# First shift and scale by TensorE in halves of 512 features, and q, k, v in halves of the contraction, in a two-layer fp32 transformer kernel

## The chip, the cores and the metric

The kernel runs on one core of a Trainium2 chip, as one launch. The metric is device time in microseconds (us). A core has TensorE (PE in the profile, with PEld for its weight loads), VectorE (DVE), ScalarE (ACT), GpSimd (POOL) and SyncE (SP), which here only issues DMAs. Each runs its own program in order, and semaphores tie them together.

## The reference

Two layers over 256 tokens of 1024 features, in float32. What matters here is the start of the first layer:

```python
mod = c @ w_ada[l] + b_ada[l]                        # c: 1 x 1024, w_ada: 1024 x 6144
sh1, sc1, gt1, sh2, sc2, gt2 = jnp.split(mod, 6, axis=-1)
h = modulate(rms_norm(x, g_pre_mix[l]), sh1, sc1)    # h * (1 + sc1) + sh1
proj = h @ w_in[l]
bg, cg, u, q, k, v, ga, gb = jnp.split(proj, ...)    # 512 columns each, ga and gb 1024
```

q, k and v feed a stick-breaking attention of 8 heads, bg, cg and u a short convolution, ga and gb gate the two. An output projection, an MLP, and then a second layer with sparse attention and a gated MLP follow. `sh1` and `sc1` are needed before the first product, `gt1` only after the first layer's `w_out`.

## The kernel before, in words

**Products.** Each large product is done in chunks of 1 MB of weights, numbered p = 0, 1, 2 and so on. SP brings chunk i of a list named `plan` into one of four `raw` buffers (L555); a buffer is used again when its last reader has let go. ACT writes `w_hi`, the chunk rounded to fp32r (`high`, L1126), DVE writes the rest, `w_lo = raw - w_hi` (`low`, L1517), and TensorE adds up three passes: w_hi by act_hi, w_hi by act_lo, w_lo by act_hi (`passes`, L596). `w_hi` and `w_lo` have three slots each, so `high(p)` waits until product p - 3 is done. After each product p, ACT and DVE take up chunk p + 3 (`high_after`, `low_after`). A product with 256 columns of weights is 8 tiles of contraction x 2 blocks x 3 passes = 48 matmuls with 256 moving columns into one bank of PSUM.

**The first products.** `in1_order` runs q, k, v (two chunks of 256 columns each, p = 0 to 5), then c, u, b, ga and gb (p = 6 to 19). Every product needs all 1024 features of h. The heads' work stands between products from p = 6 on: scores at L711, transposes at L721, outputs at L735.

**Shift and scale.** All six vectors of `mod` are made alike. DVE multiplies each row tile of `w_ada` by its element of c and adds it to `mod_acc` (L1506, L1509), two instructions of 1024 columns for each 1 MB chunk. Four chunks make one vector; TensorE then adds over the partitions with `ones` (`modulation_sum`, L633) and DVE adds the bias (`modulation`, L1545). The eight chunks of SCALE1 and SHIFT1 stand first in the plan, ahead of product 0; the other sixteen stand behind products (`n % 2`, that is after 1, 3, 5, ... 23, and four in the MLP).

**The start.** TensorE turns x, adds its squares (L642), and fills in with matmuls of the identity (`keep_busy`, L665). ACT takes the root (L1138), scales x by the scale (L1162), splits products 0 and 1, and then adds the shift and rounds to `act_hi` (L1168). POOL multiplies by the reciprocal root (L2154). DVE makes `act_lo` (L1576).

The order on ACT there, in code:

```python
high(0)
high(1)
act.wait_ge(mod_set, 2)
for k in range(DT):
    act.wait_ge(y_normed, k + 1)
    e.activation(act_hi[:, k, :], wide[1][:, k, :], ACT.Identity,
                 bias=mod[:, SHIFT1 * DT + k:SHIFT1 * DT + k + 1]).then_inc(tiles_hi, 1)
preload(ACT.Sigmoid)
```

Of the kernel before, what the change touches and what calls it, by code (L numbers as in the profile page):

```python
# [15 lines left out]
P = 128  # L16
# [54 lines left out]
def build(nc, a, out):  # L71
# [30 lines left out]
    with fixed:  # L102
# [14 lines left out]
        eps, scratch1, mean_of, rstd_out = (singles[:, 0:1], singles[:, 1:2], singles[:, 2:3], singles[:, 4:4 + TT])  # L117
# [145 lines left out]
        for name, width in (("b", CONV), ("c", CONV), ("u", CONV), ("q", ATTN), ("k", ATTN), ("v", ATTN),  # L263
# [3 lines left out]
        in1_order = [(name, i) for name in ("q", "k", "v", "c", "u", "b", "ga", "gb")  # L267
                     for i in range(in1[name].shape[1] // CHUNK_COLS)]
# [12 lines left out]
        ada_order = [(v, r) for v in (SCALE1, SHIFT1, GATE1, SHIFT2, SCALE2, GATE2) for r in range(ADA_CHUNKS)]  # L281
# [10 lines left out]

        GATE2_WITH = tuple(MLP1 + 7 + i * 10 // (ADA_CHUNKS - 1) for i in range(ADA_CHUNKS))
# [10 lines left out]
        def plan_product(source):  # L304
            n = len(product_at)
            product_at.append(len(plan))
            plan.append(("w", n, source))
            if n % 2 and n < 6 * ADA_CHUNKS or n in GATE2_WITH:
                plan_ada()

        for _ in range(2 * ADA_CHUNKS):
            plan_ada()
        for name, i in in1_order:
            plan_product(in1[name][:, i * CHUNK_COLS:(i + 1) * CHUNK_COLS])
# [32 lines left out]
        steps = [i for i, item in enumerate(plan) if item[0] != "ada"]  # L347
# [6 lines left out]
        def raw_view(i):  # L354
# [16 lines left out]
        gains_set, y_scaled, y_normed = sem("gains_set"), sem("y_scaled"), sem("y_normed")  # L371
# [40 lines left out]
        down_half, down_added, gain_applied, close_squared, bias_set = (  # L412
            sem(n) for n in ("down_half", "down_added", "gain_applied", "close_squared", "bias_set"))
# [15 lines left out]
        squared_by = (5, 9, 13)  # L429

# [26 lines left out]
        for i in range(DT // 2):  # L457
            banks.use(("x", i), squared, i + 1)
        banks.use(("mod", SCALE1), mod_set, 1)
        banks.use("rows1", cols_set, 2)  # L460
        banks.use("rows2", cols_set, 3)
        banks.use(("mod", SHIFT1), mod_set, 2)
        evacuated = {"q": qk_copied, "k": qk_copied, "v": v_copied, "c": c_copied, "u": u_gated, "b": b_copied,
                     "ga": gated, "gb": gated}
        counted = {}
        for p, (name, i) in enumerate(in1_order):
            s = evacuated[name]
            counted[id(s)] = counted.get(id(s), 0) + 1
            banks.use(p, s, counted[id(s)])
            if p == 2 * ADA_CHUNKS - 1:  # L470
                banks.use(("mod", GATE1), mod_set, 3)
# [8 lines left out]
        banks.use(("mod", SHIFT2), mod_set, 4)  # L480
        banks.use(("mod", SCALE2), mod_set, 5)
# [3 lines left out]
        for i in range(DT // 2):  # L485
            banks.use(("mlp_out", i), branch2_set, 2 * i + 2)
            if i == 0:
                banks.use(("mod", GATE2), mod_set, 6)
# [48 lines left out]
        mod_no = {v: n for n, v in enumerate((SCALE1, SHIFT1, GATE1, SHIFT2, SCALE2, GATE2))}  # L537
# [4 lines left out]
        def sync_program(e):  # L542
# [20 lines left out]
        def tensor_program(e):  # L563
# [42 lines left out]

            def product_low_last(p, o, hi, lo, ready):

                for parts in ((0, 1), (2,)):
                    for k in range(DT):  # L610
                        passes(p, o, hi, lo, ready, k, 0, True, True, parts=parts)
# [79 lines left out]
            for i in range(DT // 2):  # L691
                sum_tiles((2 * i, 2 * i + 1), i == 0, i == DT // 2 - 1, (squared, i + 1))
            keep_busy(8, bank[O_BANK])
# [45 lines left out]

            for p, (name, i) in enumerate(in1_order):  # L740
                step = p - 6
# [10 lines left out]
                if p in (1, 2):  # L752
# [1524 lines left out]
```

## Time and profile before

| | |
|---|---|
| time, median of 3 runs | 771.2 us (770.83 to 771.45) |
| span of the profiled execution | 769.0 us |
| time less span, taken for the profiled execution too | 2.2 us |
| PE busy | 737.8 us (96%) |
| DVE, ACT, POOL busy | 508.3 us (66%), 369.1 us (48%), 80.3 us (10%) |
| mean granted TensorE clock | 0.981 |
| read from HBM | 144.57 MB |

The span runs from the first to the last instruction; the profile gives no other time for its execution, so its own time is taken as the span plus the 2.2 us. Busy time is the sum over the span. A matmul on plain float32 operands is run as two instructions, so eight such matmuls stand as x16. The end of a matmul is modelled and overlaps the start of the next, so the price of one in a row is the distance between starts.

### The profile page before, as it was taken

Reading aid. Unit: us, or ns where it says so; the run is one execution under the profiler, and the core shown is the slowest. Engines: PE = TensorE matmul, PEld = TensorE weight load, DVE = VectorE, ACT = ScalarE, POOL = GpSimd, SP = SyncE. Lnnn points to the kernel's source line nnn. Section 1 sums busy time; section 2 is a strip of 40 time slices with the busy share of each in tenths; the row PEclk is TensorE's granted clock in tenths of the full one; section 3 lists DMA queues with packets and bytes.
Section 4 is the critical chain, followed back from the end, with each engine's and each line's share of the span. In section 5 each row is a group of like instructions: output and inputs, shape, how many; then the busy total and the mean of one; then the engine's idle time right before and its main releaser. Section 6 shows DMA issues by size and latency. Waiting matters only on the chain.

```text
span 769.0 us, 13566 instructions
## 1 busy us (share of the span) xinstructions
PE 737.8 (96%) x5881; PEld 703.9 (92%) x5881; DVE 508.3 (66%) x609; ACT 369.1 (48%) x508; POOL 80.3 (10%) x76
## 2 busy tenths in 40 slices
PE   4899999999999999999999999998899999999996
PEld 4899999999999999999999999786699999999884
DVE  4998689687575777754446989865655665556361
ACT  3453444444545455534336365676654544444341
POOL 1500111003000000000014000013000322221001
PEclk9799999999999999999999989999899999999998
DMA  9989866877605777766551551605334665664511
GB/s 341 375 284 326 273 203 209 284 279 226 222 5 190 246 225 250 239 223 214 173 169 55 181 170 35 196 24 177 97 107 141 214 217 176 216 187 170 190 57 55
DMA packets 118335, 146.49 MB, mean 191 GB/s; under 512 B 4004, under 2 KB 103556, under 8 KB 118276
## 3 DMA queue, kind: packets, MB, share of 16 engines
q1 hardware_dynamic: 116912, 143.58, 56.7%
q10 hardware_dynamic: 1364, 2.05, 0.8%
q8 instruction: 46, 0.75, 0.4%
q14 instruction: 13, 0.11, 0.0%
HBM read 144.57 MB, written 1.05 MB: 189 GB/s over the span
## 4 chain that ended last, share of the span: by engine, by line
PE 77%; DVE 15%; ACT 4%; DMA 2%; issue 2%; POOLq 0%; SPq 0%; DVEq 0%; ACTq 0%
PE bank L596 56%; PE bank L1087 8%; DVE w_lo L1517 6%; ACT w_hi L1126 3%; DVE mod_acc L1509 3%; PE bank L778 3%; DMA raw<-in_w_ada 2%; DVE wide L1786 1%; PE bank L878 1%; PE bank L880 1%; PE bank L656 1%; PE bank L633 1%; PE bank L858 1%; PE bank L897 1%; PE bank L642 1%
## 5 line engine op out<-in xcount | busy, mean ns | idle before, releaser
L1517 DVE TENSOR_TENSOR w_lo<-raw,w_hi 128x2048 fp32r<-128x2048 f32 x108 | 243.3, 2258 | 119.3 <-ACT w_hi L1126 119.2
L1126 ACT ACTIVATE w_hi<-raw 128x2048 fp32r<-128x2048 f32 x110 | 206.9, 1885 | 222.2 <-PE bank L596 175.8
L596 PE MATMUL bank<-act_hi,w_hi 128*128 128x256 f32 x816 | 228.1, 281 | 0.4 <-ACT act_hi L1283 0.3
L596 PE MATMUL bank<-act_lo,w_hi 128*128 128x256 f32 x816 | 225.9, 279 | 1.4 <-DVE act_lo L1808 0.7
L596 PE MATMUL bank<-act_hi,w_lo 128*128 128x256 f32 x816 | 222.0, 278 | 0.0
L596 PEld LDWEIGHTS bank<-act_hi,w_hi 128*128 128x128 f32 x816 | 154.2, 189 | 3.4 <-issue 2.8
L596 PEld LDWEIGHTS bank<-act_lo,w_hi 128*128 128x128 f32 x816 | 153.3, 188 | 2.3 <-DVE act_lo L1808 0.9
L596 PEld LDWEIGHTS bank<-act_hi,w_lo 128*128 128x128 f32 x816 | 151.2, 188 | 0.0
L596 PE MATMUL bank<-ffn_hi,w_hi 128*128 128x256 f32 x352 | 98.1, 279 | 0.0
L596 PE MATMUL bank<-ffn_hi,w_lo 128*128 128x256 f32 x352 | 97.4, 277 | 0.6 <-DVE w_lo L1517 0.6
L596 PE MATMUL bank<-ffn_lo,w_hi 128*128 128x256 f32 x352 | 97.3, 277 | 0.0
L596 PE MATMUL bank<-hidden_hi,w_lo 128*128 128x256 f32 x256 | 70.8, 277 | 0.9 <-DVE w_lo L1517 0.9
L596 PE MATMUL bank<-hidden_hi,w_hi 128*128 128x256 f32 x256 | 71.0, 277 | 0.0
L596 PE MATMUL bank<-hidden_lo,w_hi 128*128 128x256 f32 x256 | 70.7, 276 | 0.0
L596 PEld LDWEIGHTS bank<-ffn_hi,w_lo 128*128 128x128 f32 x352 | 66.2, 188 | 0.8 <-DVE w_lo L1517 0.8
L596 PEld LDWEIGHTS bank<-ffn_lo,w_hi 128*128 128x128 f32 x352 | 66.1, 188 | 0.1
L596 PEld LDWEIGHTS bank<-ffn_hi,w_hi 128*128 128x128 f32 x352 | 66.1, 188 | 0.1
L1509 DVE SCALAR_TENSOR_TENSOR mod_acc<-raw,col_tile,mod_acc 128x1024 f32<-128x1024 f32 x42 | 55.3, 1318 | 2.4 <-DMA raw<-in_w_ada 1.2
L596 PEld LDWEIGHTS bank<-hidden_hi,w_lo 128*128 128x128 f32 x256 | 48.1, 188 | 1.1 <-DVE w_lo L1517 1.1
L596 PEld LDWEIGHTS bank<-hidden_lo,w_hi 128*128 128x128 f32 x256 | 48.1, 188 | 0.0
L596 PEld LDWEIGHTS bank<-hidden_hi,w_hi 128*128 128x128 f32 x256 | 48.1, 188 | 0.0
L2226 POOL TENSOR_TENSOR wide<-wide,rstd 128x512 f32<-128x512 f32 x11 | 28.9, 2625 | 143.8 <-ACT wide L1466 143.8
(277 smaller groups left out, 1101.7 us busy)
## 6 DMA issues: line engine op xcount, KB each, us to landing
raw<-in_w_in SPq DMA_DIRECT2D x31, 1024.0 KB, 6.1
raw<-in_w_ada SPq DMA_DIRECT2D x24, 1024.0 KB, 6.3
raw<-in_w_gate_up SPq DMA_DIRECT2D x22, 1024.0 KB, 5.1
raw<-in_w_mlp_in SPq DMA_DIRECT2D x16, 1024.0 KB, 5.4
raw<-in_w_mlp_out SPq DMA_DIRECT2D x16, 1024.0 KB, 5.2
raw<-in_w_down SPq DMA_DIRECT2D x10, 1024.0 KB, 5.1
raw<-in_w_out SPq DMA_DIRECT2D x8, 1024.0 KB, 7.0
raw<-in_w_proj_conv SPq DMA_DIRECT2D x2, 1024.0 KB, 6.0
```

What stands on the lines that cost most here:

```text
L596: i = e.matmul(dst, lhs, rhs, start=start and k == 0 and (m == 0 or second is not None) and n == 0, stop=stop and k == kt - 1 and n == 2, ...
L633: i = e.matmul(o[:, k * HD:(k + 1) * HD], acc[:, k * P:(k + 1) * P], ones[:, 0:HD], start=True, stop=True, skip_group_check=True)
L642: i = e.matmul(bank[SUMS][:, 0:T], ones[:], squares[:, k, :], start=first and n == 0, stop=last and n == len(tiles) - 1, skip_group_check= ...
L656: t = e.matmul(bank[SUMS][:, tt * HD:(tt + 1) * HD], squares[:, k, tt * P:(tt + 1) * P], mean_of.to_broadcast([P, HD]), start=k == 0 and t ...
L778: t = e.matmul(o[:, m * T:(m + 1) * T], wp[:, k, cut], ap[:, k, :], start=k == 0 and m == 0 and n == 0, stop=k == kt - 1 and n == 2, skip_ ...
L858: t = e.transpose(b[:, i * P:(i + 1) * P], score[h % IN_FLIGHT][:, at * P:(at + 1) * P], ident[:])
L878: e.matmul(b[:, 0:keys], q2[:, h, tt * P:(tt + 1) * P], ks_T[:, g, 0:keys], start=False, stop=False, skip_group_check=True)
L1087: i = e.matmul(outs[tt][:, 0:n_cols], ap[:, k0 + k, own_], wp[:, k, :], start=first and k == 0 and n == 0, stop=last and k == kt - 1 and n ...
L1126: e.activation(w_hi[slot][:, 0:kt * n_cols], raw[i % N_RAW][:, 0:kt * n_cols], ACT.Copy).then_inc(hi_split, 1)
L1509: t = e.scalar_tensor_tensor(out=acc[:], in0=src[:, k, :], scalar=cols("c", r * ADA_TILES + k, 1), in1=acc[:], op0=ALU.mult, op1=ALU.add)
L1517: e.tensor_tensor(w_lo[slot][:, 0:kt * n_cols], raw[i % N_RAW][:, 0:kt * n_cols], w_hi[slot][:, 0:kt * n_cols].bitcast(F32), ALU.subtract) ...
L2226: e.tensor_tensor(s_, s_, rstd_2, ALU.mult).then_inc(gate_pool, 1)
```

## The change

The eight chunks of SCALE1 and SHIFT1 no longer go through DVE. Each is now 512 rows x 512 columns of `w_ada` (1 MB), in the order scale, shift for features 0 to 511, then the same for 512 to 1023. For each, `feed_mod1` runs four matmuls of 512 moving float32 columns straight from `raw`, whose weights are an element column of c spread over 32 columns, each into its own 32 partitions of one bank. DVE copies the bank (`copy_mod1`), and `pick_mod1` turns it to a column and adds the four groups by four matmuls with 8 moving columns. The bias and the `1 +` are added by DVE from there. The first four chunks stand ahead of product 0, the other four ahead of product 3.

Products 0 to 5 become q, k, v over the first 512 rows of the contraction and then q, k, v over the last 512, each 512 columns wide, in six banks. q and k use 256 moving columns as before; v has 512 moving columns. Product 0 runs its three passes one after the other over all its tiles. On ACT, `high(2)` stands ahead of the second half of scale and shift, and `high(3)` behind it; on DVE `low(3)` stands behind it. The multiplication by the reciprocal root moves from POOL (8 instructions of 256 columns) to DVE (4 of 512), ahead of the first copy. The other sixteen `w_ada` chunks stay on DVE; twelve of them move from behind products 1, 3, ... 23 to behind 6, 8, 10, 12, 14, 16, 17, 18, 19, 20, 21, 22, and the sum for GATE1 from after product 7 to after product 12.

```diff
-        in1_order = [(name, i) for name in ("q", "k", "v", "c", "u", "b", "ga", "gb")
-                     for i in range(in1[name].shape[1] // CHUNK_COLS)]
+        in1_order = [(name, i) for i in range(2) for name in ("q", "k", "v")]
+        in1_order += [(name, i) for name in ("c", "u", "b", "ga", "gb")
+                      for i in range(in1[name].shape[1] // CHUNK_COLS)]
...
+        first_mod = [(half, v, r) for half in range(2) for v in (SCALE1, SHIFT1) for r in range(2)]
+        ADA_WITH = (6, 8, 10, 12, 14, 16, 17, 18, 19, 20, 21, 22)
...
+                    elif before == "mod":
+                        sp.wait_ge(mod1_fed, m + 1)
...
+            def feed_mod1(n):
+                half, v, r = first_mod[n]
+                o, i = bank[MOD1_BANKS[half][n // 2 % 2]], mod_at[n]
...
+                for j in range(HALF_ROWS):
+                    t = e.matmul(o[32 * j:32 * (j + 1), :], cols("c", r * HALF_ROWS + j, 1).to_broadcast([P, 32]),
+                                 raw_view(i)[:, j, :], start=r == 0, stop=r == 1, skip_group_check=True)
+                t.then_inc(mod1_fed, 1)
+            def pick_mod1(m):
+                o = bank[MOD1_BANKS[m // 2][m % 2]]
+                pe.wait_ge(*mod1(f"copied{m}"))
+                for k in range(HALF_ROWS):
+                    t = e.matmul(o[:, k * 8:(k + 1) * 8], mod1_rows[m][:, k * P:(k + 1) * P], pick.to_broadcast([P, 8]),
+                                 start=True, stop=True, skip_group_check=True)
+                t.then_inc(mod1_picked, 1)
+            keep_busy(4, bank[O_BANK])
+            feed_mod1(0)
             keep_busy(8, bank[O_BANK])
-            modulation_sum(SCALE1)
+            feed_mod1(1)
             transpose_rows(1)
             transpose_rows(2)
-            keep_busy(30, bank[O_BANK])
-            modulation_sum(SHIFT1)
-            keep_busy(5, bank[O_BANK])
+            pick_mod1(0)
+            feed_mod1(2)
+            keep_busy(8, bank[O_BANK])
+            feed_mod1(3)
+            keep_busy(4, bank[O_BANK])
+            pick_mod1(1)
+            keep_busy(6, bank[O_BANK])
...
+            for part in range(3):
+                half_product(0, Q_BANKS, 0, (part,), by_row)
+            half_product(1, K_BANKS, 0, (0, 1, 2), by_row)
+            feed_mod1(4)
+            feed_mod1(5)
+            half_values(2, 0, between={(0, 2): partial(pick_mod1, 2), (1, 0): feed_shift, (1, 3): partial(pick_mod1, 3)})
+            half_product(3, Q_BANKS, 1, (0, 1, 2), by_row)
+            half_product(4, K_BANKS, 1, (0, 1, 2), by_bank)
+            half_values(5, 1)
...
# ACT
+            scale_half(0)
             high(0)
+            shift_half(0)
+            preload(ACT.Sigmoid)
             high(1)
+            high(2)
+            scale_half(1)
+            shift_half(1)
...
# DVE
             reciprocal(0)
+            for i in range(DT // 2):
+                e.tensor_tensor(wide[1][:, s2, :], x_T[:, s2, :], rstd_2, ALU.mult).then_inc(y_normed, 1)
+            copy_mod1(0)
             transpose_rows(1)
             transpose_rows(2)
+            scale_half(0)
+            copy_mod1(1)
+            shift_half(0)
+            first_low(0)
+            stream_to(product_at[2])
+            copy_mod1(2)
+            scale_half(1)
+            copy_mod1(3)
+            shift_half(1)
+            first_low(1)
...
             for p, (name, i) in enumerate(in1_order):
+                if p < 6:
+                    low_after(product_at[p])
+                    if p >= 3:
+                        first_copies(p)
+                    continue
```

## Rows read from the trace of the kernel before

**Rows 1.** The page: busy time, and the granted TensorE clock in 40 slices.
```profile
PE 737.8 (96%) x5881; PEld 703.9 (92%) x5881; DVE 508.3 (66%) x609; ACT 369.1 (48%) x508; POOL 80.3 (10%) x76
...
PEclk9799999999999999999999989999899999999998
```

**Rows 2.** The chain that ended last in time: start, length, what.
```profile
2.94 12.58 DMA raw<-in_w_ada
...
38.16 34.41 PE bank L596 x287
72.57 0.86 PE bank L711 x8
...
701.14 60.44 PE bank L1087 x264
```

**Rows 3.** Timeline of the start: start, length, engine, line, instruction.
```profile
13.64 1.95 PE L665 MATMUL bank<-ident 128*128 128x128 f32 x16
...
15.19 0.47 ACT L1138 ACTIVATE rms<-bank,singles 128x256 f32<-128x256 f32 x1
...
20.78 1.75 DVE L1550 RECIPROCAL rstd<-rms 128x256 f32<-128x256 f32 x1
...
20.92 3.67 PE L633 MATMUL bank<-ones,mod_acc 128*128 128x64 f32 x16 [5.33 <-DVE mod_acc L1509]
...
27.64 3.30 ACT L1162 ACTIVATE wide<-x_T,scale 128x256 f32<-128x256 f32 x8 [11.98 <-DVE scale L1567]
...
34.26 1.90 PE L633 MATMUL bank<-ones,mod_acc 128*128 128x64 f32 x16
...
36.66 3.46 ACT L1168 ACTIVATE act_hi<-wide,mod 128x256 fp32r<-128x256 f32 x8 [0.55 <-DVE mod L1545]
```

**Rows 4.** Stretches: length, busy time and instructions of each engine, granted clock, DMA share, GB/s.
```profile
18.00:20.00 2.00, 0.00 (x0) 0.00 (x0) 1.86 (x3) 0.00 (x0) 0.00 (x0) 1.00 1.03 410
20.00:22.00 2.00, 1.08 (x5) 1.08 (x6) 2.00 (x2) 0.00 (x0) 0.00 (x0) 0.51 1.03 410
```

**Rows 5.** One stretch, instructions of L596 alone: PE, PEld, clock, DMA.
```profile
44.14:72.34 28.20, 28.20 (x242) 28.20 (x240) 1.00 0.99 334
```

**Rows 6.** Groups by form: busy us, mean ns | idle before, releaser.
```profile
L1517 DVE TENSOR_TENSOR w_lo<-raw,w_hi 128x2048 fp32r<-128x2048 f32 x105 | 240.4, 2295 | 114.6 <-ACT w_hi L1126 114.5
...
L1742 DVE TENSOR_TENSOR x_T<-x_T,wide 128x512 f32<-128x512 f32 x8 | 5.5, 702 | 0.0
...
L1769 DVE SCALAR_TENSOR_TENSOR act_lo<-wide,mod,act_hi 128x256 fp32r<-128x256 f32 x8 | 3.6, 476 | 0.0
...
L1126 ACT ACTIVATE w_hi<-raw 128x2048 fp32r<-128x2048 f32 x107 | 204.4, 1914 | 215.1 <-PE bank L596 175.8 <-PE bank L1087 16.9 <-DMA raw<-in_w_in 13.6
L1116 ACT ACT_TABLE_LOAD x11 | 14.1, 1283 | 0.2
```

**Rows 7.** Timeline of PE around one L735 at 95 us; the second answer ends at 95.40.
```profile
94.92 0.49 PE L721 MATMUL bank<-ident,weight 128*128 128x128 f32 x3
95.34 0.87 PE L735 MATMUL bank<-weight_T,v_nat 128*64 128x256 f32 x8
96.14 0.39 PE L596 MATMUL bank<-act_hi,w_hi 128*128 128x256 f32 x1
...
95.34 0.44 PE L735 MATMUL bank<-weight_T,v_nat 128*64 128x256 f32 x2
```

**Rows 8.** Timeline of PE, plain float32 weights chunk as moving operand.
```profile
480.85 1.95 PE L914 MATMUL bank<-raw,cmp_in 128*79 128x256 f32 x8
```

**Rows 9.** DMA issues: KB each, median us from issue to landing.
```profile
raw<-in_w_ada SPq DMA_DIRECT2D x24, 1024.0 KB, 6.3
```

**Rows 10.** Timeline of DVE where the moved chunks will stand, and that stretch.
```profile
154.54 0.69 DVE L1610 TENSOR_TENSOR mixed_lo<-conv_y,mixed_hi 128x512 fp32r<-128x512 f32 x1 [4.03 <-ACT mixed_hi L1206]
155.15 2.60 DVE L1509 SCALAR_TENSOR_TENSOR mod_acc<-raw,col_tile,mod_acc 128x1024 f32<-128x1024 f32 x2
...
160.00:170.00 10.00, 10.00 (x87) 10.00 (x87) 8.22 (x6) 5.33 (x5) 0.00 (x0) 1.00 1.03 379
```

More of the change, by code:

```diff
@@ L280, in build @@
         ADA_CHUNKS = DT // ADA_TILES
[L281 removed]
+        ada_order = [(v, r) for v in (GATE1, SHIFT2, SCALE2, GATE2) for r in range(ADA_CHUNKS)]
+        first_mod = [(half, v, r) for half in range(2) for v in (SCALE1, SHIFT1) for r in range(2)]
         IN1, PC = 0, 20
@@ L536, in build @@
         S_BANKS, T_BANK, O_BANK = (4, 5), 6, 7
-        mod_no = {v: n for n, v in enumerate((SCALE1, SHIFT1, GATE1, SHIFT2, SCALE2, GATE2))}
+        mod_no = {v: n for n, v in enumerate((GATE1, SHIFT2, SCALE2, GATE2))}
+        mod1_rows = [mod_acc[n // 2][:, n % 2 * HALF_COLS:(n % 2 + 1) * HALF_COLS] for n in range(4)]
         EXT_I, ROWS_SET, TABLES, K_ROWS, Q_BASE = 2, 10, 18, 22, 23
@@ L738, in stick_output, with half_product @@
                             t.then_inc(stick_out, 1)
+            def half_product(p, outs, half, parts, order, between={}):
+                for n_at, (j, k) in enumerate(order):
+                    if n_at in between:
+                        between[n_at]()
+                    kt, n_cols = tiles_of(p)
+                    wh = w_hi[p % N_SPLIT][:].rearrange("p (k c) -> p k c", k=kt)
+                    wl = w_lo[p % N_SPLIT][:].rearrange("p (k c) -> p k c", k=kt)
+                    row = half * HALF_ROWS + k
+                    for m in range(CHUNK_COLS // P):
+                        cut = slice(j * CHUNK_COLS + m * P, j * CHUNK_COLS + (m + 1) * P)
+                        for n, (wp, ap) in enumerate(((wh, act_hi), (wh, act_lo), (wl, act_hi))):
+                            if n not in parts:
+                                continue
+                            if n == 0:
+                                pe.wait_ge(hi_split, p + 1)
+                                pe.wait_ge(*ready_h1[row][0])
+                            elif n == 1:
+                                pe.wait_ge(*ready_h1[row][1])
+                            else:
+                                pe.wait_ge(*low_ready(p))
+                            t = e.matmul(bank[outs[j]][:, m * T:(m + 1) * T], wp[:, k, cut], ap[:, row, :],
+                                         start=row == 0 and m == 0 and n == 0, stop=row == DT - 1 and n == 2,
+                                         skip_group_check=True)
+                if 2 in parts:
+                    t.then_inc(product_done, 1)
@@ new lines, in half_values @@
+            def half_values(p, half, between={}):
+                outs = [start_bank(("v", tt)) for tt in range(TT)]
+                kt, n_cols = tiles_of(p)
+                wh = w_hi[p % N_SPLIT][:].rearrange("p (k c) -> p k c", k=kt)
+                wl = w_lo[p % N_SPLIT][:].rearrange("p (k c) -> p k c", k=kt)
+                for tt in range(TT):
+                    for k in range(kt):
+                        if (tt, k) in between:
+                            between[tt, k]()
+                        row = half * HALF_ROWS + k
+                        for n, (ap, wp) in enumerate(((act_hi, wh), (act_lo, wh), (act_hi, wl))):
+                            if n == 0:
+                                pe.wait_ge(hi_split, p + 1)
+                                pe.wait_ge(*ready_h1[row][0])
+                            elif n == 1:
+                                pe.wait_ge(*ready_h1[row][1])
+                            else:
+                                pe.wait_ge(*low_ready(p))
+                            t = e.matmul(outs[tt][:, 0:n_cols], ap[:, row, tt * P:(tt + 1) * P], wp[:, k, :],
+                                         start=row == 0 and n == 0, stop=row == DT - 1 and n == 2, skip_group_check=True)
+                    if row == DT - 1 and tt == 0:
+                        t.then_inc(token_half, 1)
+                t.then_inc(product_done, 1)
```

211 lines of the change are left out of this document (130 added, 81 removed).

## The prediction, made before the changed kernel was seen

> **What bounds the kernel now.** The page comes first: TensorE is busy 96% of the span [rows 1], so only two things can move the time, the moment at which its stream of products begins and what stands or waits inside the stream. The chain of waits says what sets the beginning. It runs through the landing of `w_ada` up to 15.5 us, then through DVE's multiplications, and reaches TensorE at 38.16; from there 34.41 us of L596 follow without a break, and the sixth product ends where the scores begin, at 72.57 [rows 2]. That moment is my reference: what the changed kernel has done by its own sixth product decides, since the rest is the same work. The timeline of the start shows that TensorE itself has little to do before: turning x, the sums to 13.64, then filler, an idle stretch of 5.33 us, sums and filler again [rows 3]. So the eight DVE chunks are the bound of the start, and the change goes to the right place.
>
> **Durations.** A product of 256-column matmuls: 28.20 us for 240 weight loads, 0.1175 each, 5.65 for 48 [rows 5]. With 512 columns 60.44 / 264 = 0.229 [rows 2], 5.5 for the 24 of a v half. `high` 1.91, `low` 2.29, a 512-column DVE copy or product 0.70, `act_lo` 0.48, a table load 1.28 and 0.2 for the instruction behind it [rows 6]. Scale and shift on ACT: 3.30 / 8 = 0.41 and 3.46 / 8 = 0.43 [rows 3]. A filler matmul: 1.95 / 16, less the overhang of the last, 0.112 for each of its two instructions, so 0.9 for four and 1.8 for eight [rows 3].
>
> **The price of a feed.** The trace has no matmul with 32 columns of weights, so I bound it. A plain float32 matmul with 256 moving columns takes 0.22 an instruction: 1.95 for eight [rows 8], less the 0.2 by which a last one overhangs (two that start together stand as 0.44 in [rows 7]), hence 0.43 with 512 columns and 0.86 for the two of one matmul. Four matmuls one after the other: 3.45. But the heads' outputs, with 64 columns of weights into two halves of the partitions, run side by side: two had begun before 95.40, and all eight (four with 256 columns, four with 128) fit between 95.34 and 96.14 [rows 7], 0.80 where one after the other they would need 4 x 0.22 + 4 x 0.11 = 1.3. Four groups at once would give 0.86, two at a time 1.7. I take four at once, since halves overlap fully there. The row also shows the price of going in and out: three transposes stand from 94.92, the last starting near 95.14, and the first output starts at 95.34, against 0.11 between transposes, and 0.1 again on leaving. With both, 1.05 a feed. The Trainium skill (TensorEngine Tiling, Column Tiling and Key Properties) allows four groups for 32 columns and says that a change of tiling mode drains TensorE; by the drain a feed is 1.05, by the speedup alone 0.86, and the gaps in the row agree with the drain. A pick is eight instructions with 128-column weights. `modulation_sum` takes 1.90 / 16 less its overhang, 0.112 each [rows 3]; with 8 columns in place of 64 somewhat less, and I take 0.75, bounds 0.5 and 0.95.
>
> **Until product 0.** Sums end and filler begins at 13.64; four fillers 14.55, feed 0 15.6, eight fillers 17.4, feed 1 18.45. DMA brings 404 GB/s or so (410 in [rows 4]), 2.6 us for 1 MB, and a chunk takes 6.3 from issue [rows 9]; four chunks and x are there by 18.2, chunk 0 of `w_in` is issued after feed 0 and there near 21. Next is late: DVE. The root ends at 15.66 and its reciprocal, 1.75, at 17.4 [rows 3]; the four multiplications taken from POOL stand ahead of the first copy, 2.8, to 20.25, copy 20.95. So TensorE idles 2 us, then pick 0 21.7, feed 2 22.75, filler 24.55, feed 3 25.6, filler 26.5, pick 1 27.25, six fillers 28.6. The shift is ready for ACT at 27.6, the first `act_hi` at 28.1. Product 0 starts at **28.7**.
>
> **From product 0 to product 3.** ACT has `high(0)` behind it by then, writes four `act_hi` to 29.4, loads the table to 30.9, then `high(1)` 32.8 and `high(2)` 34.7. DVE: `act_lo` 30.1, `low(0)` 32.4, `low(1)` (behind `high(1)`) 35.1, `low(2)` 37.4. Product 0 runs its passes apart and needs `low(0)` only at 32.5: it ends at 34.35. Today it ends at 72.57 - 5 x 5.65 = 44.3, so **9.95 us are gained** up to here. Product 1 mixes its passes: two matmuls, then 0.5 of wait for `low(1)`, end 40.5. Feeds 4 and 5 (their raw slots came free at 25.6 and 32.4, so they have landed) 42.6. The v half with two picks and feeds 6 and 7 inside: 5.5 + 1.5 + 2.1, end 51.7, pick 3 ending at 51.0, with 0.7 of v behind it.
>
> **The new wait.** In program order `high(3)` stands behind the second half of scale and shift on ACT, and `low(3)` behind that half's `act_lo` on DVE. The chain from pick 3 is: 0.25 to wake DVE, 0.2 for the shift, 1.8 for four `act_hi`, 1.91 for `high(3)`, 2.29 for `low(3)`, so 57.5. Product 3 mixes its passes and stops after two matmuls. Only 0.7 + 0.24 of TensorE's work covers a chain of 6.5: **5.5 us of wait**, whatever a feed costs. Queued behind `high(3)` are `high(4)` and `high(5)`, behind `low(3)` are `low(4)` (59.8), `low(5)` and the copies of q and k. Product 3 ends at 62.9, product 4 at 68.55, the v half at 74.05. `low(6)`, the q copies, one moved `w_ada` chunk (2.1) and `low(7)` (to 73.0) stand ahead of the k copies on DVE, which end at 74.4, so the scores wait 0.35 and begin at 74.45 against 72.57.
>
> **The sum**, on that path: product 0's end -9.95; four feeds in the stream +4.2; two picks +1.5; two v halves -0.3; waits +0.5, +5.5, +0.35. That is +1.8; by the clock times above 74.45 - 72.57 = +1.9, which I take.
>
> **Later.** Twelve `w_ada` chunks stand closer together: seven of them behind products 16 to 22 where four stood. DVE gets three more, 7.8 us at 2.60 each, and DMA 2 MB for each 5.65 us, 2 x 2.6 = 5.2, just under. Idle before L1610 alone is 4.03 there, and DVE is busy 8.22 of 10 us around the densest part [rows 10], so most is hidden; if DVE falls behind by its slack, up to 2 us come out. I take +0.5, bounds 0 and 2. GATE1's sum only changes place. POOL's eight instructions were not on the stream's path. Total +2.4: the span 771.4, and with the 2.2 us around it (median less span) **773.6 us**, 0.3% slower. Its own range, with picks from 0.5 to 0.95, later crowding 0 to 2 and half a microsecond of hops, is 771.8 to 776.
>
> **Rivals.** *Cheap extras (not slower).* TensorE drains nothing between feeds and products, and a pick costs 0.5: six of the feeds (two behind the copy, four in the stream) save 0.2 each, four picks 0.25 each, 2.2 in all, and without the later crowding the sum is -0.3: 770.9, within 0.2%. It decides if a feed is under 0.9 and a pick under 0.55. The 0.112 of an instruction with full weights speaks against the pick, the gaps at 95 us against the feed; more than that, from slack I don't see, would make it faster. *Two groups at a time.* Then a feed is 1.9: 0.85 more for six feeds, +5.1, 778.7. For it: nothing in the trace ran four. *The clock falls.* After 5.33 us of idleness the granted clock was 0.51 in the next stretch [rows 3, 4], its lower level of 1.2 GHz, and slice 2 of the page at 0.7 means some 11 us at that level [rows 1]. In the changed kernel TensorE idles 2 us to 20.95 and then runs picks with few columns. If it falls there, the 7.7 us of work to product 0 take 5 more: 778.6. Against it: the idleness is less than half as long. *The wait at product 3 is not there*, because `act_hi` and `high(3)` overlap more than their rows say: 773.6 - 5.5 = 768.1. Their order on two in-order engines speaks against it.
>
> **Chances.** Forecast 0.52, cheap extras 0.19, two groups or one at a time 0.11, clock 0.09, no wait 0.09. A measurement of this kernel tells 0.2% (1.5 us) from no change, so faster is under 769.7 and slower over 772.7. The forecast's own range lies above 772.7 for 0.41 of its 0.52, and with the two slow rivals that makes slower 0.61; the other 0.11 of it and 0.13 of cheap extras make same 0.24; the rest of cheap extras, 0.06, and no wait make faster 0.15. The range takes in the forecast, cheap extras, two groups and the clock: 770.3 to 779; outside lie no wait and one group at a time (six times 2.4 more, 788).
>
> **What would show it.** Right: product 0 near 29; the passes of a feed starting in fours, 1.05 a feed; a wait of about 5.5 on `w_hi` L1126 and `w_lo` L1517 just before the fourth product; scores first near 74.5. Wrong: feeds of 2 us; a granted clock of 0.5 behind 20 us; no wait ahead of product 3; TensorE waiting for `w_lo` between 140 and 180 us, where none is now.

## The result, and the profile after

The changed kernel takes **790.92 us** (median of 4 runs, 788.74 to 793.29); the kernel before takes 771.33 beside it. The ratio is 1.0271 [1.0242, 1.03]: 2.7% slower, where 0.3% was forecast. The direction is right, and the size is missed by 17 us, well outside the range of 770.3 to 779. The profiled run took 792.17 us, with a span of 790.4 against 769.0 (1.8 us lie around the span here, where 2.2 were taken), so 21.4 us have to be accounted for.

The page of the changed kernel, busy time and the granted clock in 40 slices:

```profile
PE 749.9 (95%) x5871; PEld 704.4 (89%) x5871; DVE 492.5 (62%) x604; ACT 368.5 (47%) x508; POOL 71.7 (9%) x68
...
PEclk9998999998999999999999989999799999999999
```

TensorE has fewer instructions and is busy longer than in [rows 1], since at the lower clock the same work counts as more busy time. The loss isn't one of work but of waits and of the clock around them. TensorE's waits that the kernel before doesn't have are these (line, releaser, total, times, longest):

```profile
PE bank L901 <- ACT wide L1337: 3.7, 1, 3.7
PE bank L816 <- ACT w_hi L1249: 3.0, 1, 3.0
PE bank L626 <- DVE wide L1859: 2.6, 1, 2.6
PE bank L816 <- DVE w_lo L1652: 2.0, 2, 1.5
PE bank L738 <- DVE mod_acc L1705: 1.5, 1, 1.5
PE bank L626 <- DVE wide L2189: 1.3, 1, 1.3
...
PE bank L776 <- POOL weight L2342: 1.2, 1, 1.2
```

Three of these were forecast: pick 0 (L738) and the two ahead of product 3 (L816). The others, at the first projection (L901), at the first layer's output product (L626 behind L1859), at its like in the second layer (L2189) and at the transposes (L776), were not.

**A ruler.** Each chunk has one `high`, so the start of `high(p)` against the same p before shows where the stream falls behind. The **lag** is that difference. It reads 7.8 us at p = 16 (135.7 against 127.9), 14.0 at p = 26 (204.3 against 190.3), 19.1 at p = 27 (215.9 against 196.8), the same up to p = 61, 21.5 at p = 78 (602.3 against 580.9), and stays there to the end. Hence +7.8 from the start and the first products, +6.2 between products 16 and 26, +5.1 from one reading to the next, +2.4 in the second layer.

**The start.** TensorE's timeline, in order of time (start, us, line, shape; in brackets the idle time before it and who ended it):

```profile
14.97 1.05 PE L689 MATMUL bank<-ident 128*128 128x128 f32 x8
15.95 1.07 PE L729 MATMUL bank<-raw,col_tile 128*32 128x512 f32 x8
16.95 2.05 PE L689 MATMUL bank<-ident 128*128 128x128 f32 x16
...
21.96 1.06 PE L738 MATMUL bank<-singles,mod_acc 128*128 128x8 f32 x8 [1.53 <-DVE mod_acc L1705]
22.95 1.93 PE L729 MATMUL bank<-raw,col_tile 128*32 128x512 f32 x8
...
31.68 2.07 PE L816 MATMUL bank<-act_hi,w_hi 128*128 128x256 f32 x16
...
58.06 0.58 PE L816 MATMUL bank<-act_hi,w_hi 128*128 128x256 f32 x1 [2.99 <-ACT w_hi L1249]
...
60.39 0.58 PE L816 MATMUL bank<-act_hi,w_lo 128*128 128x256 f32 x1 [1.53 <-DVE w_lo L1652]
```

A feed is 1.00 from start to start (15.95 to 16.95); the one at 22.95 takes 1.86 for the same eight instructions. There the granted clock had fallen: it is 0.5, its lower level of 1.2 GHz, for 3.4 us from 23.0, and again for 6.8 us from 57.1, within the waits for product 3. The chain of waits through product 3 (start, us, what):

```profile
53.48 0.81 PE bank L738 x8
...
55.72 0.49 ACT act_hi L1293
56.21 1.81 ACT w_hi L1249
58.04 2.30 DVE w_lo L1652
60.39 12.59 PE bank L816 x94
72.98 5.51 PE bank L841 x24
...
85.08 2.88 POOL weight L2342 x2
```

The chain is the forecast one, step for step: last pick, `act_hi`, `high(3)`, `low(3)`, products 3 and 4, the v half. The last row is the wait that it didn't name: POOL's weights for the heads, behind DVE's copies of v, hold up the transposes until 88.00.

**Products 16 to 26.** First the chain from 156 us, then stretches (all engines, the columns of [rows 4]; the first is DVE's time from one chunk to the next), then two instructions of ACT:

```profile
156.39 6.95 DMA raw<-in_w_proj_conv
...
163.36 1.85 ACT w_hi L1249
...
165.66 0.63 ACT mixed_hi L1341
...
166.31 0.69 DVE mixed_lo L1778
167.00 0.68 DVE mod_acc L1641
...
167.70 1.28 DVE mod_acc L1644
168.99 2.21 DVE w_lo L1652
171.22 6.99 DMA raw<-in_w_proj_attn
178.23 1.92 ACT w_hi L1249
```

```profile
145.20:151.56 6.36, 6.36 (x56) 6.36 (x55) 6.25 (x8) 2.40 (x2) 0.00 (x0) 1.00 0.42 126
...
160.00:170.00 10.00, 10.00 (x87) 10.00 (x87) 6.71 (x7) 2.92 (x3) 0.00 (x0) 1.00 0.77 275
170.00:180.00 10.00, 6.73 (x55) 6.32 (x54) 8.35 (x6) 4.17 (x3) 0.00 (x0) 1.00 1.00 325
180.00:190.00 10.00, 9.32 (x56) 9.32 (x57) 9.46 (x8) 4.66 (x6) 0.00 (x0) 0.66 1.08 362
```

```profile
178.23 1.91 ACT L1249 ACTIVATE w_hi<-raw 128x2048 fp32r<-128x2048 f32 x1 [5.43 <-DMA raw<-in_w_proj_attn]
180.05 0.58 ACT L1337 ACTIVATE wide<-bank 128x512 f32<-128x512 f32 x1
```

The chain is a loop. A landing releases `high`, `high` stands on ACT ahead of `mixed_hi` (L1341), DVE waits for that before `mixed_lo`, then does the moved `w_ada` chunk (1.96) and `low` (2.21), and only the end of `low` frees the `raw` buffer for the next transfer, which lands 7.0 later. It turns once in 14.87 us (163.36 to 178.23). DVE is idle for 3.3 us between 160 and 170, yet its 1.96 us lie on the chain. Ahead of that, from 145.20 to 163.06, it has next to no idle time: a product with a chunk behind it takes DVE 6.36 us, of which 6.25 are busy, and TensorE 5.65. So two things are at work here, a DVE that has more to do than there is time for, and the loop.

TensorE is idle for 3.7 us ahead of 180.68, and not for want of weights: it is at product 21, whose `low` ended at 175.91. It waits for a bank. Up to here the banks go round in a ring of three, and the third of the projection's is the one that product 19 had. Its reader on ACT (L1337) stands behind `high(22)`, and that waits until 178.21 for a landing, so ACT sits idle for 5.43 us with the bank's reader behind it. This is how the late landing gets to TensorE. The clock is 0.5 for 6.8 us from 180.0, which is the 0.66 of the last stretch.

**The output product.** The merges of the first output product's input (L1859, the last DVE readers of the attention banks) run to 202.7, and L626 waits 2.6 for the last of them, from 199.9; the clock is 0.5 for 3.4 us from 203.9. DVE does a `low` (199.82, 2.28 us) ahead of that last merge (202.02). The kernel before has the same order on DVE, and no wait here at all.

### The profile page after: what moved, and what is told of

Same layout as the page of the kernel before. It is cut to its first block, busy times and chain, and to the rows that moved or that the text cites. A ratio compares the mean times of both kernels' runs of the same rounds, so it can differ in the third digit from the quotient of the medians.

```text
span 790.4 us, 13529 instructions
## 1 busy us (share of the span) xinstructions
PE 749.9 (95%) x5871; PEld 704.4 (89%) x5871; DVE 492.5 (62%) x604; ACT 368.5 (47%) x508; POOL 71.7 (9%) x68
## 3 DMA queue, kind: packets, MB, share of 16 engines
HBM read 144.57 MB, written 1.05 MB: 184 GB/s over the span
## 4 chain that ended last, share of the span: by engine, by line
PE 67%; DVE 18%; ACT 7%; issue 4%; DMA 2%; POOL 1%; POOLq 0%; SPq 0%; ACTq 0%; DVEq 0%
PE bank L626 44%; PE bank L1210 8%; DVE w_lo L1652 7%; ACT w_hi L1249 5%; PE bank L816 2%; DVE mod_acc L1644 2%; DVE wide L2014 2%; PE bank L841 1%; PE bank L666 1%; DVE wide L1968 1%; DVE score L2098 1%; DMA raw<-in_w_proj_attn 1%; PE bank L680 1%; DMA raw<-in_w_proj_conv 1%; PE bank L657 1%
## 5 line engine op out<-in xcount | busy, mean ns | idle before, releaser
L626 PE MATMUL bank<-act_hi,w_hi 128*128 128x256 f32 x752 | 212.9, 283 | 4.3 <-DVE wide L1859 2.6
L626 PE MATMUL bank<-act_lo,w_hi 128*128 128x256 f32 x752 | 210.2, 280 | 0.9 <-DVE act_lo L1990 0.7
L626 PE MATMUL bank<-act_hi,w_lo 128*128 128x256 f32 x752 | 210.2, 279 | 0.0
L626 PEld LDWEIGHTS bank<-act_hi,w_hi 128*128 128x128 f32 x752 | 142.3, 189 | 7.4 <-DVE wide L1859 2.8
L626 PEld LDWEIGHTS bank<-act_lo,w_hi 128*128 128x128 f32 x752 | 142.2, 189 | 1.4 <-DVE act_lo L1990 0.9
L626 PEld LDWEIGHTS bank<-act_hi,w_lo 128*128 128x128 f32 x752 | 142.7, 190 | 0.0
L626 PE MATMUL bank<-ffn_hi,w_hi 128*128 128x256 f32 x352 | 98.1, 279 | 0.0
L626 PE MATMUL bank<-ffn_hi,w_lo 128*128 128x256 f32 x352 | 97.5, 277 | 0.4 <-DVE w_lo L1652 0.4
L626 PE MATMUL bank<-ffn_lo,w_hi 128*128 128x256 f32 x352 | 97.3, 277 | 0.0
L626 PE MATMUL bank<-hidden_hi,w_lo 128*128 128x256 f32 x256 | 70.8, 277 | 0.9 <-DVE w_lo L1652 0.9
L626 PE MATMUL bank<-hidden_hi,w_hi 128*128 128x256 f32 x256 | 71.0, 277 | 0.0
L626 PE MATMUL bank<-hidden_lo,w_hi 128*128 128x256 f32 x256 | 70.7, 276 | 0.0
L626 PEld LDWEIGHTS bank<-ffn_hi,w_lo 128*128 128x128 f32 x352 | 66.2, 188 | 0.6 <-DVE w_lo L1652 0.6
L626 PEld LDWEIGHTS bank<-ffn_lo,w_hi 128*128 128x128 f32 x352 | 66.1, 188 | 0.1
L626 PEld LDWEIGHTS bank<-ffn_hi,w_hi 128*128 128x128 f32 x352 | 66.1, 188 | 0.1
L626 PEld LDWEIGHTS bank<-hidden_hi,w_lo 128*128 128x128 f32 x256 | 48.1, 188 | 1.1 <-DVE w_lo L1652 1.1
L626 PEld LDWEIGHTS bank<-hidden_lo,w_hi 128*128 128x128 f32 x256 | 48.1, 188 | 0.0
L626 PEld LDWEIGHTS bank<-hidden_hi,w_hi 128*128 128x128 f32 x256 | 48.1, 188 | 0.0
L1644 DVE SCALAR_TENSOR_TENSOR mod_acc<-raw,col_tile,mod_acc 128x1024 f32<-128x1024 f32 x28 | 36.4, 1301 | 0.6
```

Source lines behind the costliest of these rows:

```text
L626: i = e.matmul(dst, lhs, rhs, start=start and k == 0 and (m == 0 or second is not None) and n == 0, stop=stop and k == kt - 1 and n == 2, ...
L1644: t = e.scalar_tensor_tensor(out=acc[:], in0=src[:, k, :], scalar=cols("c", r * ADA_TILES + k, 1), in1=acc[:], op0=ALU.mult, op1=ALU.add)
```

## The experiments

The ratios are against the kernel before, run beside it; "lag" is the ruler above.

**e1: only the moved order, in the kernel before.**

```diff
+        ADA_WITH = (6, 8, 10, 12, 14, 16, 17, 18, 19, 20, 21, 22)
...
-            if n % 2 and n < 6 * ADA_CHUNKS or n in GATE2_WITH:
+            if n in ADA_WITH or n in GATE2_WITH:
...
-                if p == 2 * ADA_CHUNKS - 1:
+                if p == ADA_WITH[ADA_CHUNKS - 1]:
```

> The kernel before, with one thing of the change: its twelve w_ada chunks for GATE1, SHIFT2 and SCALE2 stand behind products 6, 8, 10, 12, 14, 16 to 22, and the GATE1 sum behind product 12. Theory A (my new one, from the profile of the changed kernel: from product 16 on the ring of four raw buffers turns slower than TensorE takes its products, and 9 to 13 us of waits come out between products 16 and 26): 7 to 13 us slower than before, TensorE waiting at the first projection (L778) and at the first L596 of w_out. Rival B (the crowding hurts only because the changed kernel comes to it late and with its copies behind): within 2 us of before. My prediction's term was +0.5.

Measured: 777.03 us, 1.0092 [1.007, 1.0115]. The lag is 0.5 at p = 16, 6.1 at p = 26, 7.2 at the end, and the new wait is the one of the changed kernel under its own line numbers:

```profile
PE bank L779 <- ACT wide L1203: 3.8, 1, 3.8
```

The clock is at 0.5 for 6.8 us from 171.7, within that wait. So the crowded order alone costs 6.8 us by the medians (777.03 against 770.22) and 5.6 in the lag between p = 16 and p = 26, without anything of the new start. That is just under the 7 to 13 expected; the prediction had 0.5 for it.

**e2: the moved chunks spread out, in the changed kernel.**

```diff
-        ADA_WITH = (6, 8, 10, 12, 14, 16, 17, 18, 19, 20, 21, 22)
+        ADA_WITH = (3, 5, 6, 7, 9, 11, 13, 15, 17, 19, 21, 23)
```

> The changed kernel with those twelve chunks behind products 3, 5, 6, 7, 9, 11, 13, 15, 17, 19, 21, 23 and the GATE1 sum behind product 7. Theory A: the lag against before stays at the 6 us that it has at product 15, about 777 to 779 us, and no wait over 1 us on TensorE between 140 and 210 us. Rival B: the waits move but stay, 786 or more. Either way the waits ahead of product 3 (5.3 us) stay.

Measured: 788.7 us, 1.0251 [1.0218, 1.0284]: a miss, though the part in question went as expected. The lag no longer grows between p = 16 (12.3) and p = 26 (11.1). But it had grown to 12 us beforehand, at another place. The wait, and the chain that leads to it:

```profile
PE bank L766 <- DVE k_T L1803: 4.0, 1, 4.0
```

```profile
60.76 1.29 DVE mod_acc L1644
...
62.07 8.67 DMA raw<-in_w_in
...
70.76 1.93 ACT w_hi L1249
...
80.83 1.29 DVE k_T L1803 x2
```

It is the loop once more. DVE lets go of the chunk behind product 3 at 62.05, only then is the transfer of product 6's weights issued, and it lands 8.67 us later; `high(6)`, `low(6)` and the copies behind them come late with it. The k copies start at 80.83 where the changed kernel has 77.23, the scores wait 4.0 us for them, and the clock falls to 0.5 for 6.8 us from 80.7.

**e3: the second DVE instruction of each of the twelve chunks on 8 columns instead of 1024.** It leaves out half of the products of `w_ada` with c in those chunks.

```diff
+                        n_ = 8 if k and n < 12 else D
-                        t = e.scalar_tensor_tensor(out=acc[:], in0=src[:, k, :], scalar=..., in1=acc[:], ...)
+                        t = e.scalar_tensor_tensor(out=acc[:, 0:n_], in0=src[:, k, 0:n_], scalar=...,
+                                                   in1=acc[:, 0:n_], ...)
```

> The changed kernel, but of the two DVE instructions of each of those twelve chunks the second works on 8 columns in place of 1024 (it leaves out half of the sums for GATE1, SHIFT2 and SCALE2): 1.2 us of DVE less for each chunk, the same DMA. Three theories of the loss between products 16 and 26. T1, DVE has too much work: most of the 9 to 13 us come back. T2, the transfers of 2 MB for each product are too much: nothing comes back. T3, one turn of the ring (landing, high, low, chunk, next issue, one after the other) takes 14.8 us for two products of 11.3: each turn gets 1.2 shorter, 3 to 5 us come back.

Measured: 784.07 us, 1.0194 [1.0137, 1.0252]. The lag is 8.1 at p = 16 and 8.8 at p = 26, and the wait at the first projection is gone. 5.5 of the 6.2 us come back, where 3 to 5 were expected from the loop alone and most of it from a DVE with too much work.

**e4: only half of each of the twelve chunks transferred, DVE's work left whole.** It leaves out the transfer of the other half of those chunks, and what DVE then reads there is old data.

```diff
+                k_ = ADA_TILES // 2 if kind == "ada" and n < 12 else source.shape[0] // P
-                e.dma_start(raw_view(i), source.rearrange(...)).then_inc(raw_landed[i % N_RAW], 16)
+                e.dma_start(raw_view(i)[:, 0:k_, :], source.rearrange(...)[:, 0:k_, :]).then_inc(...)
```

> The changed kernel, but only the first half of each of those twelve chunks is transferred (512 KB; DVE then works on the full chunk, half of it old data, so half of the sums for GATE1, SHIFT2 and SCALE2 are left out of the right result): the same DVE work, 1.3 us of DMA less for each. T1: nothing comes back. T2: most of the 9 to 13 us. T3: the weights chunk behind lands 1.3 us sooner in each turn, 3 to 5 us come back, much like the run with less DVE work.

Measured: 792.78 us, 1.0301 [1.0263, 1.0339]; lag 7.9, 14.4 and 19.5 at p = 16, 26 and 27. Nothing comes back. Even the landing that follows a halved chunk isn't earlier: issued at 156.58, there at 163.74, where the changed kernel has 156.39 and 163.34. With e3 this shows that DVE's added work is the price, and the bytes of `w_ada` are not. It doesn't show in which way: as a link of the loop, or because DVE has more work than time. The loop was expected to give 3 to 5 us back here through earlier landings, and no landing was earlier. No run separates the two, and none puts L1337 ahead of `high` on ACT. Had the bank been free, product 21 would have run from 176.8 to some 182.4 (an estimate, from 5.65 a product), and `low(22)` ends at 182.46, so little of the 3.7 would be left at that place.

**e5: the banks set back.** The banks of PSUM are dealt out in program order by `banks.use`, one entry after the other, from a ring of three (0 to 2) up to the attention's projection and of seven (all but 3) from the output product on. Each entry waits for the last reader of the entry that had the bank before. The change makes five entries fewer (33 stand ahead of the first output product, where 38 did), so every later entry lands in another bank. The first two output products, which start together, had banks 5 and 6, free for long; now they have 7 and 0, and bank 0 is read last of all, by the fourth merge (L1859). The experiment moves the counter on:

```diff
         for i in range(DT // 2):
             banks.use((PA, i), attn_part_set, i + 1)
+        banks.pos += 5
```

> The changed kernel with the counter of the bank plan moved on by five before w_out, so that every bank from w_out on is the one that the kernel before uses. Theory C: the changed kernel makes five fewer entries in the plan, by which the second bank of w_out is the one that the last merge still reads; TensorE waits 2.9 us there and loses some 1.7 more to the lower clock, and 2 us again at the second layer's output. Then 4 to 7 us faster than the changed kernel, 784 to 787, and the lag against before no longer grows between products 26 and 27. Rival: that wait comes of DVE running late, and stays: 790.

Measured: 785.18 us, 1.0188 [1.0141, 1.0235]. The lag is 12.1 at p = 26 and 12.3 at p = 27 where it was 14.0 and 19.1: the step of 5.1 is 0.2. The 1.3 us wait in the second layer (L2189) is gone too. Besides, this profile was ahead of the changed kernel's from the start, by something that the edit doesn't touch: its squares are summed in 3.65 us rather than 4.83, pick 0 starts at 20.90 rather than 21.96, the clock doesn't fall at 23 us, and product 0 starts at 29.01 rather than 31.68.

**e6: `high(3)` and `low(3)` out of the way of scale and shift.**

```diff
 # ACT
             scale_half(1)
+            high(3)
             shift_half(1)
 # the loop behind it then skips high(3)
...
 # DVE
             copy_mod1(3)
+            stream_to(product_at[3])
             shift_half(1)
```

> The changed kernel with high(3) ahead of the second shift on ACT and low(3) ahead of it on DVE. Theory of my prediction: the 5.3 us of waits ahead of product 3 are the order on the two engines; about 1 us of them stays. The idle stretch then no longer lowers the clock (it is at 0.5 for 6.8 us from 57.1 on, which costs 3.4). Together 4 to 7.5 us less when the scores begin, and as much in the end if nothing later is waited for instead. Rival: the landing of chunk 3 or the copies behind it wait next, and under 2 us are gained.

Measured: 784.46 us, 1.0187 [1.0129, 1.0246]. Neither wait stands ahead of product 3, the clock stays up at 57 us, and the lag at p = 7 is 0.8 where it was 6.1. That is 5.3 us. The later steps stay: from 2.9 at p = 16 to 9.8 at p = 26 and 14.9 at p = 27.

**e7: twenty filler matmuls ahead of product 3, in the wait.**

```diff
+            keep_busy(20, bank[banks.bank["scale1"]])
             half_product(3, Q_BANKS, 1, (0, 1, 2), by_row)
```

> The changed kernel with 20 filler matmuls (4.5 us) on TensorE between product 2 and product 3, in a bank that nothing uses then. The waits stay as long as they are. If idleness lowers the clock, the stretch at 0.5 from 57 us on is gone and product 3 ends 3.4 us earlier; if not, nothing changes. Little of it need reach the end, since the scores wait for the copies of k.

Measured: 787.37 us, 1.0224 [1.0168, 1.028]. TensorE alone, stretches of the changed kernel and then of this one (busy time, granted clock, share of DMA, GB/s):

```profile
56.00:62.00 6.00, 2.40 (x9) 0.59 0.52 138
60.00:70.00 10.00, 9.61 (x70) 0.80 0.83 272
```

```profile
56.00:62.00 6.00, 5.38 (x47) 1.00 0.59 186
60.00:70.00 10.00, 10.00 (x82) 1.00 0.97 318
```

82 matmuls instead of 70 in the same 10 us. Set against e5, whose start also ran without the fall at 23 us, product 3 ends 2.1 earlier, not the 3.4 that a stretch of 6.8 us at half clock would give, because part of that stretch lies in the wait itself (57.1 to 60.39). So the idle time brings the fall, and the fall costs about 2 us on top of the wait.

**e10: only other places for the chunks.**

```diff
-        ADA_WITH = (6, 8, 10, 12, 14, 16, 17, 18, 19, 20, 21, 22)
+        ADA_WITH = (6, 8, 9, 10, 11, 13, 15, 17, 19, 21, 23, 25)
```

> The changed kernel with one edit, the twelve moved chunks behind products 6, 8, 9, 10, 11, 13, 15, 17, 19, 21, 23, 25. Theory A: the lag against before, 7.8 us at product 16, does not grow until product 26 (in the changed kernel it grows by 6), the 4 us wait at the first projection is gone; the 5 us at w_out stay, since the banks are left as they are. 783 to 786. Rival: the waits come out elsewhere, 789.

Measured: 782.02 us, 1.0144 [1.0095, 1.0192]. The lag is 5.1 from p = 15 to p = 26 without a step, then 9.9 at p = 27. This is what e2 was meant to show. Of the 8.9 us between the two kernels at p = 26, 6.2 are the step that is gone; the other 2.7 were there at p = 16, since this profile too ran without the fall at 23 us, as e5 and e7 did.

**e8: e5, e6 and e10 together.**

> The changed kernel with three edits: the banks as in the kernel before, high(3) and low(3) earlier, and the twelve moved chunks behind products 6, 8, 9, 10, 11, 13, 15, 17, 19, 21, 23, 25. If the three losses are separate: 21.5 less 7 (banks) less 6 (order) less 9 (crowding) leaves the changed kernel within 3 us of before, 768 to 774. If they share their time: 776 or more.

Measured in 12 runs: 772.95 us, 1.0028 [1.0001, 1.0055]. Of the 19.6 us between the medians 17 are gone. The profile is that of the longest of the twelve (776.19). Its lag is 1.7 from p = 16 to p = 65, and 5.5 at the end: in the second layer the clock is 0.5 for 10.2 and 13.7 us where the kernel before has 6.8 and 6.8.

**e9: the bank step in the kernel before.** The counter moved by 4, so that the output product gets banks 1 and 2, those of the last two attention parts.

```diff
         for i in range(DT // 2):
             banks.use((PA, i), attn_part_set, i + 1)
+        banks.pos += 4
```

> The kernel before with the counter of the bank plan moved on by four ahead of w_out, so that the two banks of w_out's first products are those of the last two merges, and all later banks turn with it. Theory C (a bank that is still read, nothing else): TensorE waits some 2 to 3 us at the first matmul of w_out's second product, the clock may fall for 3.4 us more, 2 to 6 us slower than before. Rival: in the kernel before the merges are done in time, no wait, 0.

Measured in 10 runs: 777.51 us, 1.0089 [1.0064, 1.0114]; the lag goes from -1.6 at p = 26 to 4.4 at p = 27. Its waits:

```profile
PE bank L597 <- DVE wide L1678: 3.3, 1, 3.3
PE bank L878 <- ACT gate L1333: 2.5, 1, 2.5
```

One number in a plan of banks is worth 0.9% in a kernel of which not an instruction has changed. The second wait says that this shift hits one more place, so the 7 us are the price of two.

**e11: the start reordered as well.** e8, and besides: pick 0 behind feeds 2 and 3 and without filler there; DVE copies the second bank ahead of the first scaling; ACT loads its table and does `high(0)` before scaling; the copies of q and k stand ahead of the `low` of the same product.

```diff
-            pick_mod1(0)
             feed_mod1(2)
-            keep_busy(8, bank[O_BANK])
             feed_mod1(3)
-            keep_busy(4, bank[O_BANK])
+            pick_mod1(0)
             pick_mod1(1)
...
# DVE
-            scale_half(0)
             copy_mod1(1)
+            scale_half(0)
```

> The three edits together, and three more: feeds 2 and 3 run ahead of the first pick, in TensorE's idle 1.8 us, without filler; on ACT the table load and high(0) stand ahead of the first scale; q, k and v are copied ahead of the next low. By the rows of the changed kernel the first act_hi comes at 26.5 in place of 31.1, the wait at product 1 (0.8) and that of the transposes at 80 us (1.5) go: 5 to 6 us less than with three edits, 766 to 769, faster than before by 0.2 to 0.6%. Rival: with fewer filler matmuls the clock is at 0.5 around 25 us for 7 to 10 us, and nothing is gained: 771 to 774.

Measured in 12 runs: **767.79 us**, 0.9953 [0.9929, 0.9978], below both kernels. TensorE's timeline and stretches at the start:

```profile
20.57 1.92 PE L730 MATMUL bank<-raw,col_tile 128*32 128x512 f32 x16
22.42 1.95 PE L739 MATMUL bank<-singles,mod_acc 128*128 128x8 f32 x16
24.23 1.58 PE L690 MATMUL bank<-ident 128*128 128x128 f32 x12
26.46 2.07 PE L815 MATMUL bank<-act_hi,w_hi 128*128 128x256 f32 x16 [0.65 <-ACT act_hi L1292]
```

```profile
20.00:30.00 10.00, 9.35 (x81) 1.00 1.01 360
60.00:70.00 10.00, 10.00 (x65) 1.00 0.96 336
```

Product 0 starts at 26.46, 5.2 earlier than in the changed kernel, and the clock doesn't fall. The lag is -4.6 from p = 15 to p = 65. Half of it goes in the second layer, where one stretch of 17.1 us at half clock begins at 531.6; it ends at -2.3. So the idea of the change, with its start in order and its side effects undone, is worth 4.6 us up to the second layer, and 3.6 by the ratio in all.

## Why the prediction was right and wrong

**What bounds the start: right.** The eight DVE chunks did, and taking them away makes the stream begin 6.5 us earlier (31.68 against 38.16 in [rows 2]), and 11.7 in e11.

**The price of a feed and a pick: right.** A feed is 1.00, two in a row 1.85, forecast 1.05 each with 0.2 of going in and out; a pick in the stream 0.81, forecast 0.75. The eight matmuls of a feed:

```profile
L729 PE MATMUL bank<-raw,col_tile x8: 592/604/617, 16.0 to 16.4; 128*32 128x512 f32 x8
```

All eight last 0.6 us and start within 0.4: four groups run at once. The Trainium skill (TensorEngine Tiling (Array Packing), Key Properties) says that tiles execute independently and that a change of mode drains TensorE. The overlap agrees with the first; 1.00 with filler around the feed against 1.85 for two in a row leaves 0.15 for going in and out (0.85 a feed), which agrees with the second. Both rivals on the price of a feed are out.

**Product 0's start: 3 us late.** Forecast 28.7, measured 31.68. The idle time ahead of pick 0 is 1.5 (forecast 2). The squares were summed in 4.83 us instead of the 3.62 before, so filler begins at 14.97 and not at 13.64; and the clock fell at 23.0 for 3.4 us. Against e5, where neither happened, these two are 2.7 at product 0's start (31.68 against 29.01): 1.1 of it is there at pick 0 (21.96 against 20.90), and the other 1.6 is the fall. The fall was a rival, with a chance of 0.09 and a price of 5 us: it came in 6 of the 9 profiles with this start, in four of them for 3.4 us, at a third of the price, and in e3 and e6 for 6.8 us, at two thirds (product 0 at 32.22 in e3, with pick 0 at 20.92, and at 29.01 in e5, with pick 0 at 20.90). Without the two, product 0 starts at 29.0 against the forecast 28.7.

**The wait ahead of product 3: right, but not whole.** Starts of matmuls are 3.4 and 1.9 apart, 5.3 in all, of which some 5.0 are wait, against the forecast 5.5. What the prediction didn't price is the clock that falls with it (e7): 2.1.

**The wait at the transposes: missed.** 1.2 us, 1.4 in the lag (6.1 at p = 9, 7.5 at p = 10). DVE's queue had been followed to the k copies but not on to the copies of v, the scans and POOL's weights.

The forecast +1.9 on this path, 2.6 of late sums and fall at the start (e5's lead at product 4: 4.2 less 1.6 of lag), 2.1 of clock at 57 us and 1.4 here give 8.0, against the 7.8 of product 16. The 0.35 us for the k copies, part of the +1.9, didn't come: the scores begin at 78.57 without a wait, forecast 74.45.

**The first step that failed.** "Idle before L1610 alone is 4.03 there, and DVE is busy 8.22 of 10 us around the densest part [rows 10], so most is hidden; if DVE falls behind by its slack, up to 2 us come out. I take +0.5, bounds 0 and 2." It measured +6.2, and +5.6 by itself (e1). The idle time before L1610 was read as slack. In this place it is the return leg of a loop: DVE waits for `mixed_hi`, that for `high`, that for the landing, and the landing for DVE's own `low`. Nor was DVE's time for a product set against TensorE's, and it is 6.36 us against 5.65 there. That the crowded places are the cause is shown by e1 and e10, and that it is their work on DVE by e3; how much of it goes through the loop and how much is plain overload stays open. TensorE feels it once, as 3.7 us for a bank whose reader stands behind a late `high`, and loses the rest to the clock. The sign named for this, TensorE waiting for `w_lo` between 140 and 180 us, showed as 0.2 us at 171.25; the wait that counts was for a bank, which the prediction had not looked at. The forecast's other term there, 5.2 us of DMA in each 5.65, was no part of it (e4).

**The second step, which was not there at all.** "The rest is the same work", the prediction says. It is, but not in the same banks. 5.1 us at product 27 and most of the 2.4 of the second layer come from a plan that deals out banks in order, from which the diff takes five entries (e5, e9). For the second layer this is read from three profiles whose stretch at half clock there is 6.8 us, as in the kernel before: between p = 74 and p = 78 the lag grows by 1.8 in e3 and 1.9 in e6, and by nothing in e5. The lines of the diff that did this were the `q, k, v` that leave `banks.use` and the fixed `MOD1_BANKS`.

**What stays open.** Beside the bank, the second layer has a stretch at half clock of 10.2 us where 6.8 stood. Such stretches differ from one profile to the next (3.4 to 17.1 us there, over the eleven experiments), so their part is not settled, and neither is why e11 has the longest. Whether another order on ACT would have spared the wait for the bank is not tested either. Since the effects overlap, their prices taken singly (9.8 for the places, 6.4 for the banks, 6.5 for the order at product 3, by the medians' ratios) come to more than the 17 to 19 that they give together.

## What to carry to other kernels

Idle time of an in-order engine is slack only if what it waits for doesn't depend on that engine: follow the wait all the way back, through the buffer ring, before hiding work in it, and set the engine's whole time for a step against that of the engine that bounds the kernel. Where a reader of a bank stands behind something that waits for a landing, the landing holds up the bank too. When a diff takes entries out of anything that is dealt out in order (banks, slots, counters), write down the assignment before and after for every later user, since a shift of the ring can cost more than the edit gives. And price a wait inside TensorE's stream with the stretch at half clock that may follow it, here 1.6 to 3.2 us on top of waits of 1.5 to 5.

## What was not expected of the hardware

With waits of 1.5 to 4 us inside a stream at full clock came stretches of 3.4 to 17.1 us at 0.5, which began inside the wait (57.1, 171.7, 180.0) or some 1 us behind it (23.0, 203.9). The same wait at the same place gave different lengths, or none, in different kernels. The clearest case stands in the second layer, where TensorE waits for a score of DVE's:

```profile
PE bank L981 <- DVE score L2098: 5.8, 2, 4.2
```

The longer of the two waits (L858 in the kernel before) is 4.2 us in all thirteen profiles, and the stretch at 0.5 with it is 3.4 us in e9 and e10, 6.8 in the kernel before, 10.2 in the changed one and 17.1 in e11.

The fall at the start has a sign ahead of it: with the start of the change, the clock fell at 21 to 23 us in the six profiles in which the squares took 3.9 to 4.9 us to sum, and not in the three in which they took 3.62 to 3.65. That time isn't the change's doing: the kernel before has 3.62 in its profile, and e9, whose start is that of the kernel before, 4.66. e11 summed them in 4.70 and had no fall, which speaks for its denser start, from one profile. The Trainium skill (TensorE: Matmul & The Clock Gate, Part 1: The HAM clock gate) gives two levels, 1.2 and 2.4 GHz; the granted clock of 0.5 and 1.00 in the stretches above agrees.

Halving the `w_ada` transfers that stand between the weight chunks brought the landing behind one no further forward (7.16 us from issue against 6.95), though DMA's share in that time went down from 0.95 to 0.74.
